# Last tile scaled by TensorE instead of VectorE, and expert blocks in two turns of 24, in a one-core decoder layer

## The reference

```
logits = h @ router_w + router_b;  top 4 of 32 experts for each token
each expert: act = (clip(up)+1) * min(gate,7) * sigmoid(1.702*gate);  out = act @ w_down + b_down
y = layer_norm(ALPHA*h + sum over the 4 of gate weight * out, ln2_g, ln2_b)
layer_norm(x) = (x - mean) * rsqrt(mean((x - mean)**2) + 1e-5) * g + b
```

## Time and profile before

| | |
|---|---|
| median of 3 runs | 1552.15 us (1551.94 to 1555.91) |
| the profiled execution's own time | 1555.71 us |
| its span | 1554.0 us |
| mean granted TensorE clock | 0.991 |

### The profile page before, as it was taken

The page is one execution under the profiler, slowest core; times in us unless marked ns, Lnnn a source line. Parts: engine busy times, 40 slices in busy tenths (PEclk is TensorE's granted clock), DMA queues, the critical chain, the costliest instruction groups (busy, mean ns, idle before and its releaser), DMA issues.

```text
span 1554.0 us, 21022 instructions
## 1 busy us (share of the span) xinstructions
PE 1488.0 (96%) x8226; PEld 758.5 (49%) x8227; DVE 490.3 (32%) x955; ACT 277.8 (18%) x618; POOL 110.7 (7%) x98
## 2 busy tenths in 40 slices
PE   9999999999999999999999999999899899899896
PEld 6777777655677775333333333333333333333332
DVE  2651445676450036311222122122122122121123
ACT  1222435532111003201010110100100100100102
POOL 1001132010050702000000000000000000000000
PEclk9999999999999999999999999999999999999999
DMA  6346396536239764999999999999999999999995
GB/s 207 109 142 191 115 293 227 196 126 204 72 116 319 259 250 176 419 426 427 427 428 426 430 427 430 428 429 428 428 428 428 429 428 429 427 430 427 430 427 228
DMA packets 105352, 507.67 MB, mean 327 GB/s; under 512 B 7575, under 2 KB 44031, under 8 KB 80575
## 3 DMA queue, kind: packets, MB, share of 16 engines
q1 hardware_dynamic: 100938, 499.37, 80.2%
q10 hardware_dynamic: 4360, 7.55, 1.4%
HBM read 491.18 MB, written 15.72 MB: 326 GB/s over the span
## 4 chain that ended last, share of the span: by engine, by line
PE 63%; DMA 24%; DVE 1%; ACT 1%; issue 1%; DVEq 0%; SPq 0%; ACTq 0%
DMA wGU<-in_w_gu 23%; PE ps L2324 11%; PE ps L1829 11%; PE ps L2329 10%; PE ps L2311 5%; PE ps L1842 4%; PE ps L2132 3%; PE ps L2238 2%; PE ps L2146 2%; PE ps L2159 2%; PE ps L2272 2%; PE ps L2246 1%; DMA ringS<-in_ssd_proj 1%; PE ps L1905 1%; ACT xs L1273 1%
## 5 line engine op out<-in xcount | busy, mean ns | idle before, releaser
L2324 PE MATMUL ps<-wGU,xe 128*64 128x512 f32 x1536 | 342.1, 594 | 17.4 <-DMA wGU<-in_w_gu 16.6
L2329 PE MATMUL ps<-wD,aT 128*64 128x512 f32 x1024 | 226.8, 595 | 0.0
L2324 PEld LDWEIGHTS ps<-wGU,xe 128*64 128x64 f32 x1536 | 107.9, 137 | 233.0 <-issue 198.4
L1829 PE MATMUL ps<-xT,ring 128*128 128x288 f32 x704 | 181.3, 413 | 2.6 <-PEq L199 2.1
L1829 PEld LDWEIGHTS ps<-xT,ring 128*128 128x128 f32 x704 | 131.7, 191 | 43.1 <-issue 5.0
L2329 PEld LDWEIGHTS ps<-wD,aT 128*64 128x64 f32 x1024 | 70.7, 137 | 131.8 <-issue 127.9
L2311 PE MATMUL ps<-wGU,xe 128*64 128x512 f32 x512 | 121.3, 594 | 11.9 <-DMA wGU<-in_w_gu 11.9
L1725 DVE TENSOR_SCALAR sg<-sg 128x512 f32<-128x512 f32 x32 | 13.7, 427 | 334.0 <-ACT sg L1268 334.0
L1732 DVE COPY ysb<-ps 64x512 f32<-64x512 f32 x32 | 22.2, 694 | 304.0 <-PE ps L2333 304.0
L1268 ACT ACTIVATE sg<-ps 128x512 f32<-128x512 f32 x32 | 19.1, 597 | 469.7 <-PE ps L2316 469.7
L391 PE MATMUL ps<-xT,ring 128*128 128x288 f32 x320 | 78.1, 407 | 0.0
(11 more groups left out here) (476 smaller groups left out, 1452.5 us busy)
## 6 DMA issues: line engine op xcount, KB each, us to landing
wGU<-in_w_gu SPq DMA_DIRECT2D x128, 2048.0 KB, 36.8
wD<-in_w_down SPq DMA_DIRECT2D x64, 2048.0 KB, 36.9
ring<-in_w_in SPq DMA_DIRECT2D x21, 2048.0 KB, 8.8
out<-hst SPq DMA_DIRECT2D x8, 1024.0 KB, 5.8
ringS<-in_ssd_proj SPq DMA_DIRECT2D x4, 2048.0 KB, 10.3
wbuf<-prompt_A_rows ACTq DMA_DIRECT2D x16, 384.0 KB, 3.8
out<-Sb SPq DMA_DIRECT2D x2, 2048.0 KB
ring<-in_hg_proj SPq DMA_DIRECT2D x2, 2048.0 KB, 8.3
```

Of the source, the lines that this page charges most:

```text
L1829: last = m.matmul(ps[:, b, 0:T], ring[c % 2][:, k, n * P:(n + 1) * P], xT[:, k, :], start=(k == 0), stop=(k == KD - 1))
L2324: last = m.matmul(ps[half[h], bank, :], xe[:, f, hx, :], wgu[n][:, k, col + CW * h:col + CW * h + CW], start=(i == 0 and k == 0), stop=False)
L2329: last = m.matmul(ps[half[h], B_Y, :], aT[:, k, i - 4, :], wdn[n][:, k, CW * h:CW * h + CW], start=(i == 4 and k == 0), stop=False)
```

## The change

Two things are changed. VectorE and ScalarE run the expert blocks after the first two in a loop of two turns with 24 nested bodies each (turn 0 takes blocks 2 to 25, turn 1 blocks 26 to 31 and then leaves the nest at its seventh `If`); TensorE and SyncE keep eight turns of six. In the tail, `normal2(0)` is taken from VectorE. TensorE first multiplies the identity by beta into PSUM banks 0 and 1. When VectorE has the reciprocal of tile 0's root, ScalarE builds a diagonal matrix of it (`rsd`), TensorE multiplies it by the weighed tile and adds it onto beta in the same banks, and ScalarE copies both halves back to `yacc` and stores them through its own queue. SyncE stores the sample rows first, then tile 1.

```
-                with act.Fori(0, TURNS) as it:
-                    six(act, it, end - 1, lambda it, r: run(it * 6 + (r + 2), r % 2 == 1))
+                with act.Fori(0, 2) as it:
+                    six(act, it, end - 1, lambda it, r: run(it * 24 + (r + 2), r % 2 == 1), 0, 24)
...
-                with turns(dve, 0, TURNS, (dstep, 33)) as it:
+                with turns(dve, 0, 2, (dstep, 132)) as it:
...
+                act.wait_ge(f_y, 2)
+                a.mul(rsd[:], ident[:], fvar[:, 0:1]).then_inc(f_q, 1)
+                for h in range(2):
+                    cols = slice(CW * h, CW * h + CW)
+                    act.wait_ge(f_m, 3 + h)
+                    a.copy(yacc[:, 0, cols], ps[:, B_X + h, :]).then_inc(f_n, 1)
+                    act.wait_ge(f_n, 2 + h)
+                    act.dma_start(y_prompt[0, 0:P, cols], yacc[:, 0, cols]).then_inc(s_out, 16)
...
-                lstep(weigh2(0))
+                weigh2(0).then_inc(f_y, 1)
...
-                inverse(0, 0)
+                dve.wait_ge(f_q, 1)
+                v.reciprocal(fvar[:, 0:1], fvar[:, 0:1]).then_inc(f_y, 1)
...
-                normal2(0)
...
+                pe.wait_ge(m_xc, end + 2)
+                pe.wait_ge(g_ln, 16 * 12)
+                m.matmul(ps[:, B_X, :], ident[:], lnb2[:, 0:CW], start=True, stop=False)
                 pe.wait_ge(f_v, 2)
                 m.matmul(ps[:, B_Y, 1:2], selq[:], fsq[:, 2:3], start=True, stop=True).then_inc(f_m, 1)
+                m.matmul(ps[:, B_X + 1, :], ident[:], lnb2[:, CW:D], start=True, stop=False)
+                pe.wait_ge(f_q, 4)
+                for h in range(2):
+                    m.matmul(ps[:, B_X + h, :], rsd[:], yacc[:, 0, CW * h:CW * h + CW], start=False, stop=True).then_inc(f_m, 1)
```

More of the change, by code:

```diff
@@ L629, in build @@
         f_c, f_v, f_r, f_q = S("ln2_mean_ready"), S("ln2_squares_ready"), S("ln2_variance_ready"), S("ln2_rooted")
-        f_y = S("y_ready")
+        f_y = S("first_rows_weighed_scale_then_y_ready")
         lstep = Steps(S("last_dve_step"))
@@ L707, in build @@
         lnq = at("lnq", 104, [P, D])
+        rsd = at("rsd", 110, [P, P])
         junkq = at("junkq", 108, [P, 256])
@@ L723, in expert, with six @@
             return eng.value_load(tab[0:1, bass.ds(b, 1)], min_val=0, max_val=E_ - 1)
-        def six(eng, it, left, body, r=0):
-            with eng.If(it * 6 + r < left):
+        def six(eng, it, left, body, r=0, n=6):
+            with eng.If(it * n + r < left):
                 body(it, r)
-                if r < 5:
-                    six(eng, it, left, body, r + 1)
+                if r < n - 1:
+                    six(eng, it, left, body, r + 1, n)
         def gathered(k):
@@ L900, in _ @@
                     sp.dma_start(lnb4[bands[q], :], ln2_b[0, 256 * q:256 * q + 256].partition_broadcast(32)).then_inc(g_ln, 16)
[L902 to L909, removed]
+                sp.wait_ge(f_y, 3)
+                y_s = y_sample.rearrange("b s d -> (b s) d")
+                for q in range(4):
+                    sp.dma_start(y_s[:, 256 * q:256 * q + 256], yq[bands[q], :]).then_inc(s_out, 16)
+                for h in range(2):
+                    sp.wait_ge(f_y, h + 4)
+                    sp.dma_start(y_prompt[0, P:2 * P, CW * h:CW * h + CW], yacc[:, 1, CW * h:CW * h + CW]).then_inc(s_out, 16)
                 sp.wait_ge(s_out, 96 + 16 * 8)
@@ L1749, in _ @@
                 run(1, True, None)
-                with turns(dve, 0, TURNS, (dstep, 33)) as it:
-                    six(dve, it, end - 1, lambda it, r: run(it * 6 + (r + 2), r % 2 == 1, None if r % 2 else it * 3 + r // 2))
+                with turns(dve, 0, 2, (dstep, 132)) as it:
+                    six(dve, it, end - 1, lambda it, r: run(it * 24 + (r + 2), r % 2 == 1, None if r % 2 else it * 12 + r // 2), 0, 24)
                 lstep.on(dve)
```

## The result

The changed kernel takes 1558.54 us (median of 20 runs, 1555.22 to 1561.8) against 1552.14 us (1548.72 to 1557.89) before: 6.4 us more, ratio 1.004 with a 95% interval of 1.003 to 1.0049. I had forecast 1551.3 us, within a range of 1549.8 to 1554.7. The profiled execution took 1558.78 us, 3.07 us more than the profiled one of before.

A forecast was written before the change was run, and what follows sets the result against it. Weights' DMA at 427 to 429 GB/s was taken to bound the expert phase, VectorE the tail. Terms -1.32 + 0.2 + 0.28 = -0.84 us, from the 1552.15 median, gave 1551.3 us, full range 1549.8 to 1554.7.

The forecast's parts named there:

- Fewer turns inside the phase: Expert blocks: fewer VectorE loop turns, at 0.66 us each, change nothing because waits for weights cover them; term 0.
- DMA rate unchanged: Expert phase, profile after: the weights' DMA rate stays at 428 GB/s.
- the two signs that I had named for a failure: Tail: the exit takes over 3 us, or ScalarE's stores end well after SyncE's.
- The jump back: VectorE's loop between blocks 25 and 26: even 3 us more would be covered by waits for weights; term 0.
- normal2(0) off VectorE: Tail: without it weigh2(1) starts 1.32 us earlier and normal2(1) ends at 1550.01; term -1.32 us.
- The exit: Leaving VectorE's loop: jump over 18 bodies with a fetch, 2.4 us against 1.87; term +0.28, bounds 0 and +1.0.
- Rival 3: Loop exit: two fetches of 2.6 us each, 5.7 us against 1.87, net +2.6, time 1554.7; chance 12%.
- Sharing of the stores: Tail: four stores of 256 KB fall into 1.2 us instead of 3.5; term +0.2, bounds 0 and 0.6.
- The clock: Tail, TensorE's products for tile 0: full clock is kept after 1.3 us idle; at half they would take 3.9 us.
- rival 2: Tail: TensorE's clock falls before tile 0's products, whose branch ends 1.6 us late; time 1552.35, chance 13%.
- The tail's sum: Tail terms together: -1.32 + 0.2 + 0.28 = -0.84 us.
- rival 4: Expert phase: the turns were on the path and four or more at 0.66 us go; time 1548.7, chance 5%.

The follow-up runs named there:

- run 8: New tail, all loops at six, plus 1248 idle semaphore instructions as straight code on unused GpSimd: 1554.42 us against 1552.02 for the kernel before, ratio 1.0014.
- run 9: New tail, loops at six, the same 1248 idle GpSimd instructions written as a loop over 24 blocks: 1551.14 us against 1551.85 for the kernel before, ratio 0.9995.
- run 4: The changed kernel with VectorE back at eight turns of six, ScalarE kept at two turns of 24: 1549.85 us against 1550.92 for the kernel before, ratio 0.9993.
- run 6: The changed kernel with VectorE's and ScalarE's loops at four turns of 12: 1563.42 us against 1552.02 for the kernel before, ratio 1.0079.
- run 1: The changed kernel with the old loops, eight turns of six on VectorE and ScalarE: 1549.98 us against 1550.92 for the kernel before, ratio 0.9995.
- run 10: New tail, 26 idle instructions added to each ScalarE block body, eight turns of six: 1550.04 us against 1551.85 for the kernel before, ratio 0.9988.
- run 11: The changed kernel with VectorE's and ScalarE's loops at six turns of eight: 1550.19 us against 1551.85 for the kernel before, ratio 0.9991.

## Why the prediction was wrong

**The step that failed** is "Fewer turns inside the phase ... Term 0". It measured +7.06 us. I asked what the longer loop does to VectorE's own time and found cover for it, rightly. I did not ask what it does to the resource that bounds the phase. I even wrote that queue 14 would have packets all through the phase, and gave them no price, because 80 KB in 290 MB is nothing and the share of the 16 engines was full either way. But each weight piece is spread over all engines, and VectorE's pages are all taken by the same one. The eight of them took the lag from 3.2 to 10.4 us. In VectorE's copies it shows as a lateness of 1.1 us at block 15 (pages at 932 and 1017 us), then +0.8 after 1129, +0.8 after 1220, +1.0 after 1326 and +3.0 for the three at 1366, 1371 and 1428. Runs 8 and 9 show that it is the fetch that costs, and not that the fetching engine is late.

**The sign of "DMA rate unchanged"** was right and misled. Until the stream's end the mean rate is 428 to 429 GB/s in both, since the other engines go on with the pieces queued behind. In the views only the end of the stream shows the one that lags. Neither of the two signs that I had named for a failure appeared: the exit took 2.30 us, and ScalarE's last store was issued by 1553.9 us, before SyncE's (1554.2).

**The jump back** was put at up to 3 us of stall. It took 6.2, and TensorE stood for 3.9 us and worked at half clock for 3.4 us. It cost nothing that lasts, as I had argued: of 5.8 us at block 26, 3.8 were back at block 27. The cover that I named, waits for weights, was the right one.

**normal2(0) off VectorE:** term -1.32. From the fifth addition to the end of the last `normal2` it is 1547.10 to 1553.83, 6.73 us, against 8.19: -1.46.

**The exit:** I took 2.4 us for VectorE and +0.28 for the end. It took 2.30, and the fifth addition came 5.79 us after the start of the last block's copy instead of 5.34: +0.45. The reason, a fetch at the far target, has packets at 1542.3 and 1544.7 us to show for it; the addition starts at 1544.3, so only the first can have held it. ScalarE's exit took nothing at all (0.01 us against 0.96), probably because its 24 short bodies were still held (run 4, where ScalarE alone has the long loop, has no instruction packet behind 1202 us): I had given it the same fetch. Rival 3, an exit with two fetches, didn't happen here; run 6's exit (4.20 us) is over the 3.1 us where that rival decides.

**Sharing of the stores:** term +0.2, within 0 to 0.6. From VectorE's end to the end of the span it is 3.17 us against 2.67: +0.5.

**The clock:** stayed at 2.4 GHz through the `rsd` products, after 1.05 us of idle time, as taken. That was in part luck: run 9 has the same tail and the same 1.05 us, and there the granted clock was 0.50 from 1542.7 to 1546.1 and the products took 3.68 us instead of 1.98. One line of its timeline and one window:

```profile
1542.62 3.68 PE L2383 MATMUL ps<-yacc,rsd 128*128 128x512 f32 x4 [1.05 <-ACT rsd L1307]
...
1543.00:1544.00 1.00, 1.00 (x2) 0.44 (x2) 1.00 (x1) 0.00 (x0) 0.00 (x0) 0.50 0.13 33
```

Its tail is 16.0 us against 15.3 in run 1, so rival 2 came true in this one of the 12 profiled executions with the new tail, and took most of the gain. Nothing here shows what decides it. `rsd` took 0.39 us for my 0.35.

The tail's sum is -0.5 measured for -0.84. Of the rivals, two were over tenths of a microsecond, and the third, on the slower side, looked for its loss at the exit. The one that saw the loops on the path at all, rival 4, expected a gain from it. The right one, the loop's code as a load on the stream, was not among them.

The Trainium skill, "Runtime: NRT & Kernel Launch", section Instruction fetch mechanics, was weighed for the exit only. Its rule there, that a branch to a page not held stalls for the fetch, agrees with the trace at the exit and, with 6.2 us, at the jump back. It gives the memory as two pages of 16 KB. By that size the loop of six and the turns of eight fit; the turns of 12 would fit only if they lie well, and they were not held. VectorE's pages are 8 KB in the trace, though, and there the measurement decides.

**What stays open.** Why a page sets its DMA engine back by about 1.0 us when VectorE fetches it and by 0.6 to 0.7 when GpSimd or ScalarE does (runs 8 and 4), though all are 8 KB and the packets themselves last 0.33 and 0.31 us. What decides the clock in the tail. And whether the tail alone is a gain: runs 1, 4, 9, 10 and 11 have it without a loss in the phase and lie 0.5 to 1.2 parts in a thousand below before, each interval reaching 1.000 or over. The profiled tails, 15.2 to 15.6 us in four of them against 16.2, speak for about 0.9 us where the clock stays up; run 9's 16.0 speaks for next to nothing where it falls.

## What to carry to other kernels

Where a stream that uses all DMA engines sets the pace, instruction fetches are part of the load, whoever fetches: keep every engine's loop short enough to stay in its instruction memory, GpSimd's included (here some 300 instructions on VectorE did, 450 did not). Look for instruction queues in the DMA table of such a stage, at the end of the stream for a rate of one engine alone, and at the spread of a transfer's 16 signals; a mean share can't show a laggard. Count a big visible stall as a cause only if its lateness is still there some blocks later; and change a loop's form and a tail in separate runs, since here a gain of half a microsecond went with a loss of seven.

## What I had not expected of the hardware

- An 8 KB instruction page, fetched beside a stream of 428 GB/s, sets one of the 16 DMA engines back by 0.6 to 0.7 us (GpSimd's and ScalarE's, the former with nobody waiting for it) or by 1.0 us (VectorE's). The pages of any one of the three all go to the same DMA engine, and the stream pays once that one is the last.
- A jump back of 24 or of 12 bodies stalls VectorE by 6.1 to 6.2 us while the weights stream; the jump out after the stream costs 2.3 us (with three near, empty turns it was 1.86).
- ScalarE left a nest of 24 bodies within 0.01 us, against 0.96 us through three empty turns.
- TensorE's 16 KB pages go over eight DMA engines in turn: 1.5 us on the engine, 0.17 us a page for the stream.
- With the same tail and 0.8 to 1.2 us of idle time ahead of them, TensorE's `rsd` products ran at 2.4 GHz in 11 profiled executions and mostly at 1.2 GHz in one.
